# Attention value products of a two-block fp32 kernel: values as weights in split fp32r parts, probabilities moving, outputs with features on partitions

## The reference

```python
h = rmsnorm_2(x, attn_norm_g)
fq, fk, fv, f_logit, sq, sk, sv = split(h @ w_in)     # 8 + 8 heads of width 64
# forgetting attention, causal (s <= t)
p = softmax(q @ k.T / 8 + F[t] - F[s]);  o_fox = p @ v
# stick-breaking attention, strictly causal (s < t)
w = sigmoid(z) * prod_{s<j<t}(1 - sigmoid(z[t,j]));  o_sb = w @ v
o = concat(rmsnorm_2(o_fox, fox_out_g), rmsnorm_2(o_sb, sb_out_g))
x = x + o @ w_out
...
```

## Time and profile before

| | us |
|---|---|
| median of 3 runs | 2620.15 (2619.35 to 2623.75) |
| the profiled execution's own time | 2620.05 |
| span of its profile | 2618.1 |
| busy PE / DVE / ACT / POOL | 2566.8 / 1386.6 / 974.7 / 821.0 |

### The profile page before, as it was taken

How to read it: one execution, slowest core, us unless ns; L and a number is a source line. 1 busy time by engine, 2 the same in 40 slices (tenths; PEclk the granted TensorE clock), 3 DMA queues, 4 the chain that set the end, 5 groups by cost and what they waited for, 6 DMA issues and landing times. The chain is left out here.

```text
span 2618.1 us, 32424 instructions
## 1 busy us (share of the span) xinstructions
PE 2566.8 (98%) x12922; PEld 2135.6 (82%) x12922; DVE 1386.6 (53%) x1285; ACT 974.7 (37%) x1376; POOL 821.0 (31%) x339
## 2 busy tenths in 40 slices
PE   8999999999999999999999999999999999999999
PEld 4888888888788888888888888887888888888887
DVE  5864557656666753544735455465864314431454
ACT  3410044434254420023556556564144213321334
POOL 3565443433344335542111011034422222222230
PEclk9999999999999999999999999999999999999999
DMA  8222221212121153341110111131111111111111
GB/s 328 89 87 71 99 89 57 74 52 65 61 81 61 67 197 123 96 145 65 34 41 33 41 41 34 40 120 58 49 48 48 49 48 48 48 49 64 48 57 65
DMA packets 56552, 194.32 MB, mean 74 GB/s; under 512 B 6857, under 2 KB 10825, under 8 KB 55153
## 3 DMA queue, kind: packets, MB, share of 16 engines
q1 hardware_dynamic: 41312, 141.74, 16.5%
q10 hardware_dynamic: 15120, 50.90, 5.5%
HBM read 158.50 MB, written 29.92 MB: 72 GB/s over the span
## 5 line engine op out<-in xcount | busy, mean ns | idle before, releaser
L238 PE MATMUL G<-H_hi,w_hi 128*128 128x512 f32 x1616 | 502.3, 392 | 1.0 <-ACT silu_zB L724 0.7
L269 POOL TENSOR_TENSOR w_lo<-w_raw,w_hi 128x1024 fp32r<-128x1024 f32 x133 | 348.7, 2622 | 491.1 <-ACT w_hi L263 485.2
L238 PE MATMUL G<-H_lo,w_hi 128*128 128x512 f32 x1616 | 497.7, 389 | 0.0
L238 PE MATMUL G<-H_hi,w_lo 128*128 128x512 f32 x1616 | 497.6, 389 | 0.0
L264 POOL TENSOR_TENSOR w_hi<-w_raw,ones 128x1024 fp32r<-128x1024 f32 x75 | 198.2, 2642 | 593.7 <-PE G L238 472.5
L238 PEld LDWEIGHTS G<-H_lo,w_hi 128*128 128x128 f32 x1616 | 303.3, 188 | 63.4
L238 PEld LDWEIGHTS G<-H_hi,w_lo 128*128 128x128 f32 x1616 | 303.3, 188 | 63.2
L238 PEld LDWEIGHTS G<-H_hi,w_hi 128*128 128x128 f32 x1616 | 300.7, 188 | 64.4 <-issue 4.5
L1845 POOL TENSOR_TENSOR w_lo<-w_raw,w_hi 128x1024 fp32r<-128x1024 f32 x24 | 60.2, 2507 | 479.6 <-ACT w_hi L2059 479.6
L1952 PEld LDWEIGHTS G<-att_v,probsT 128*128 128x128 f32 x1152 | 146.5, 191 | 21.9 <-ACT probsT L2088 13.1
L1900 PE MATMUL G<-A_hi,w_hi 128*128 128x512 f32 x368 | 155.7, 423 | 6.6 <-DVE projected L2238 6.3
(11 more groups left out here) (528 smaller groups left out, 4733.2 us busy)
## 6 DMA issues: line engine op xcount, KB each, us to landing
w_raw<-w_in SPq DMA_DIRECT2D x65, 512.0 KB, 3.6
w_raw<-w_up SPq DMA_DIRECT2D x44, 512.0 KB, 3.6
pre_raw<-w_in SPq DMA_DIRECT2D x30, 512.0 KB, 3.6
wm<-w_mod SPq DMA_DIRECT2D x8, 1024.0 KB, 18.3
w_raw<-w_out SPq DMA_DIRECT2D x16, 512.0 KB, 3.6
w_raw<-w_down SPq DMA_DIRECT2D x16, 512.0 KB, 3.5
xT<-xT SPq DMA_DIRECT2D x8, 512.0 KB, 19.0
b_d<-silu_zB ACTq DMA_DIRECT2D x8, 512.0 KB, 2.6
```

The costliest lines, as they stand in the source:

```text
L238: mm = nc.tensor.matmul(dst[:, n * NB:n * NB + c], w[:, k, :], m[:, k, n * NB:n * NB + c], start=first, stop=last)
L269: nc.gpsimd.tensor_tensor(w_lo[:, slot, 0:kt, :], w_raw[:, slot, 0:kt, :], w_hi[:, slot, 0:kt, :].bitcast(F32), ALU.subtract).then_inc(w_r ...
```

## The change

The value product is turned round. The values of a head are split into a high and a low part of 64 columns each, which together are one 128x128 weight block in fp32r (`VP`); the transposed probabilities are split as well (`pT`, high and low) and move, 256 columns at a time for a pair of query tiles. Rows 0 to 63 of the result are the product with the high values, rows 64 to 127 that with the low values; ACT copies one half and DVE adds the other. The result has features on partitions, so `out_turned` goes. The row sum can no longer be applied to the result, so DVE scales the probabilities of f rounds before they are turned. The squares are made of 64x512 pieces and added up over the rounds; 16 one-column matmuls against ones sum them at the end. `v_turned` moves from the U banks to the score banks, and from step 14 of the round before to step 0 of the round itself. One of the normalisation rows (`R1`) goes to DRAM and comes back at the end to make room.

```diff
@@ pe
-                for c, b0, n in GROUP_AT[g]:
-                    S.wait(pe, "act", "p copied", c)
-                    for b in range(n):
-                        mm = pe.matmul(V[:, at:at + HD], pT[c % 2][:, b, :], v[:, b0 + b, own_rows(hh)], start=b0 + b == 0, stop=b0 + b == tt)
-                    S.mark("pe", "values", mm, c)
+                order = [(b, n) for b in range(tt) for n in range(2)]
+                order = order[:-1] + [(tt, 0), (tt, 1)] + order[-1:]
+                arrived = -1
+                for b, n in order:
+                    if b // 4 > arrived:
+                        arrived = b // 4
+                        S.wait(pe, "dve", "p low", GROUP_AT[g][arrived][0])
+                    c0 = P if b == tt else 0
+                    mm = pe.matmul(V[:, at + c0:at + 2 * P], VP[:, hh, b, :], pT[n][:, b, c0:2 * P], start=(b, n) == (0, 0), stop=(b, n) == order[-1])
+                S.mark("pe", "values", mm, i)
...
-                if s >= 1:
-                    values(s - 1)
-                if n == 0 and 1 <= q <= ROUNDS:
-                    v_turned(q - 1)
-                if s > TILES and s % TILES == 2:
-                    out_turned(s // TILES - 1)
+                if s >= 2 and s % 2 == 0:
+                    values(s // 2 - 1)
+                if 0 <= s < STEPS and s % TILES == 0:
+                    v_turned(s // TILES)
...
             early(0)
-            out_turned(ROUNDS - 1)
+            S.wait(pe, "dve", "squares added", STEPS // 4 - 1)
+            for x in range(2):
+                for t in range(TT):
+                    mm = pe.matmul(S2[:, x * NB + t:x * NB + t + 1], SQ[own_rows(x), t * P:(t + 1) * P], ones[own_rows(x), 0:1], start=True, stop=True)
+            S.mark("pe", "heads summed", mm)
@@ act
+            def out_half(j):
+
+                _, hh, cols = out_at(j)
+                S.wait(act, "pe", "values", 2 * j + 1)
+                if j % 4 == 0 and j:
+                    act.wait_ge(o_stored[out_row(j // 4 - 1)], 16)
+                S.mark("act", "out half", act.activation(OT[own_rows(hh), cols], V[other_rows(hh), :], ACT.Copy), j)
+
+            def square(j):
...
+                S.mark("act", "square", act.activation(dst, OT[own_rows(hh), cols], ACT.Square), j)
@@ dve
+            def made(g):
+                x, _, tt = tile_of(g)
+                w = (tt + 1) * P
+                p, n = pr[g % 2][:, 0:w], g % TILES
+                if x == "f":
+                    S.wait(v, "act", "exp", g)
+                    do("row sum", v.reciprocal(rs[:, n:n + 1], rs[:, n:n + 1]), g)
+                    me("row sum", g)
+                    do("made", v.tensor_scalar(p, p, rs[:, n:n + 1], None, ALU.mult), g)
+                else:
                     S.wait(v, "act", "taken", g)
                     me("first", g)
                     do("made", v.tensor_tensor(p, p, left[:, T - w + 1:T + 1], ALU.mult), g)
 
+            def p_low(g):
+                cols = slice(g % 2 * P, g % 2 * P + P)
+                for c, b0, n in GROUP_AT[g]:
+                    S.wait(v, "act", "p high", c)
+                    do("p low", v.tensor_tensor(pT[1][:, b0:b0 + n, cols], blocks_of(bank_of_u(("p", c)), n), pT[0][:, b0:b0 + n, cols].bitcast(F32), ALU.subtract), c)
+
+            def v_low(r):
...
+            def out_of(j):
...
+                S.wait(v, "act", "out half", j)
+                do("out", v.tensor_tensor(OT[rows, cols], V[rows, :], OT[rows, cols], ALU.add), j)
+
+            def add_squares(j):
...
+                do("squares added", v.tensor_tensor(SQ[rows, cols], SQ[rows, cols], sqt[rows, :], ALU.add), j)
...
+                if 0 <= s + 1 < STEPS:
+                    first(s + 1)
+                if s >= 1:
+                    p_low(s - 1)
+                if s >= 1 and s % TILES == 1:
+                    v_low(s // TILES)
                 if s >= 5 and s % 4 == 1:
-                    out_of((s - 5) // 4)
+                    out_of(s // 4 - 1)
+                if s >= 7 and s % 4 == 3:
+                    add_squares(s // 4 - 1)
                 if 0 <= s + 1 < STEPS:
-                    chain(s + 1)
+                    made(s + 1)
```

214 lines of the change are left out of this document (106 added, 108 removed).

## The result

The changed kernel takes 2665.88 us (median of 4 runs, 2665.14 to 2671.87) against 2620.93 of the kernel before (4 runs, 2619.35 to 2623.75): a ratio of 1.0178, interval 1.0165 to 1.0190, some 45 us more. The forecast was 2644, +24. The direction and the order of the stages came out; the size is nearly twice the one given.

What follows compares the result with a forecast made beforehand. PE was taken to set the pace before, with DVE becoming the bound in s rounds. S rounds +16, f rounds -8, last round +14 and the end +2 gave +24 on 2620.05: 2644 us, range 2614 to 2678.

Steps and rivals of the forecast that it cites:

- S rounds, +4 each: Four s rounds: DVE's work becomes the bound, 76 us against 72.0 each, bounds +1 and +8; +16 in all.
- the clock fall as a rival: Last round: PE works in bursts and drops to 1.2 GHz, +8 on the forecast, 2652 us; chance 0.04.
- F rounds, 69 us each: Three f rounds: a new DVE-ACT chain per tile, 69 against 71.7 us, -2.8 each; -8 in all.
- The last round, +14: Last attention round, without projection pieces: longer chain and scalings held by POOL, +14 us, bounds +5 and +28.
- The chain, +6: Last round: chain through the tiles with squares, splits and final low parts takes about 54 us against 47.8, +6.
- Low parts and outputs lie under the exponential: F rounds: DVE's low parts and outputs run during ACT's exponential, so they add nothing to the 45 us chain.
- The holds, +8: Last round: DVE's scalings wait for POOL's current instruction; eight narrow tiles and three wide, +3 and +5 us.
- The end, +2: After attention: one-column sums +2.7 and slower-clock matmuls +1.6, about half hidden in existing waits; +2, bounds 0 and +4.
- DVE keeps up: All rounds: slack averages out, s rounds 69, f rounds 64.5, last round 50 us; -32, 2588 us; chance 0.14.
- It evens out: All rounds: s rounds +1, f rounds -5, last round +8, within noise; chance 0.05.
- POOL holds more: Last round: each of 14 scalings loses 1.6 us and more; f rounds gain nothing; +46, 2666 us; chance 0.20.
- The matmuls don't get cheaper: Value matmuls: 0.23 us each, PE needs 8 us a round more; about +56, 2676 us; chance 0.05.

Runs made afterwards that it cites:

- x4: Changed kernel without DVE's scaling of the probabilities in f rounds, the reciprocal kept: 2645.41 us, ratio 1.0100.
- y4: Changed kernel with the scaling of the probabilities in f rounds moved from DVE to ACT: 2676.30 us, ratio 1.0214.
- x3: Changed kernel making, from the second round on, only 16 of 128 columns of each low part of the probabilities: 2642.51 us, ratio 1.0083.
- z4: Changed kernel without scaling in f rounds and with POOL splitting only 128 of 1024 columns in the last round: 2643.96 us, ratio 1.0091.
- x2: Changed kernel with POOL splitting only 128 of 1024 columns of the seven early output tiles in the last round: 2657.90 us, ratio 1.0143.
- y2: Changed kernel with POOL's last-round splits cut to 128 of 1024 columns, plus eight spare matmuls before each value product of s rounds and last round: 2657.37 us.
- z1: Changed kernel with four spare matmuls of 256 columns before each value product of the last round only: 2664.33 us, ratio 1.0171.
- z2: Kernel before, with values and transposed probabilities in fp32r, high parts alone, so each value matmul is one pass: 2570.85 us, ratio 0.9818.
- y3: Changed kernel without low parts of the probabilities, 320 value matmuls instead of 640: 2589.68 us, ratio 0.9885.
- x1: Changed kernel with four spare matmuls of 512 columns a step in the last round, before the probabilities are turned: 2670.75 us, ratio 1.0186.
- z3: Changed kernel with DVE's product or scaling of the next tile put before the low parts instead of behind them: 2787.98 us, ratio 1.0640.

## Why the prediction was right in sign and short in size

Two steps failed. The sum has no term for the clock, which the s rounds pay; and in the last round it lets the low parts lie under ACT's exponential, while PE stands there and waits for them. Of the 28 us between the forecast (+24) and the profiled execution (+52), 16 lie in the s rounds, 13 in the last round and 1 in the f rounds; the end has 0, and the earlier start gives 3 back. By the medians the miss is 21.

**PE's side** was right. Value matmuls are 0.12 us apart (1452.16 to 1452.28), 640 of them. PE had to lose its place as the bound, and did: in the s round it is busy 66.7 of 77.2 us by the profile, against 69.1 of 72.0.

**DVE in s rounds**: right. 68.0 us forecast; the durations in the round from 1388.9 add up to 68.4. The profile's 64.5 is less because a record can overlap the next (the scan of 1449.54, above, ends at 1451.30, the low part starts at 1451.21), so busy time is the smaller number. The low parts of 512 columns take 0.68 us, taken as 0.69 from the earlier trace rows.

**S rounds, +4 each**: at full clock the later ones would be 75.5 us, +3.5 on 72.0, by the steps above. Measured were 77.2, 79.9 and 81.6. What failed is that the sum has no term for the clock in s rounds. The forecast had 63 us of work for PE in a round of 76, so 13 us of waits, and had the clock fall as a rival, but for the last round alone and with a chance of 0.04, because "in these rows the clock fell after one-column matmuls only". That sentence was false of the trace: the wait of 2.32 us in the first round, above, was there to be read, and a table by stretch of the kernel before, which I had and did not put among, gives 0.98 for 1255 to 1322. Had I asked what came before each low stretch of the clock, the rival would have become a term; its size was not to be had from one such row. By the estimate of 75.5 the clock costs 1.7 + 4.4 + 6.1 us in the three later s rounds and some 2 in the first: 14 of the 16 us that s rounds have above the +16 forecast.

**F rounds, 69 us each**: 69.2, 69.5 and 69.9. Right, and for the reason given: the chain through the tile sets them (x4 shortens the round by up to 3 us, y4 lengthens it by 4), the low parts lie beside it (x3: nothing). But the scaling and two of the handovers were 11 us of that chain (16 x 0.71), and x4 wins at most 3 without the scaling: that the total came out is in part luck.

**The last round, +14**: measured +27.3. Three parts.
- The chain, +6: with POOL quiet and the clock at 0.97 the round takes 59.6 us, +13. The failed step is "Low parts and outputs lie under the exponential": true of f rounds, where x3 finds nothing, false of the last, where it finds 9.0 us (clock included). With no pieces of the projection between, PE stands at each value product until the low part is there (21.5 us in nine waits), and the low part stands behind the next sum. The scaling's part was counted too high (11 us, z4 against x2: 4.3), so what low parts and waits add is more than the difference of 7. I carried a statement about a covered stage into one without cover.
- The holds, +8: DVE is busy 10.0 us more because of them, so the size of the hold was nearly right, the scalings were held, as said, and low parts escape; the squares, which the forecast did not name, are held too. The profiled rounds differ by 12.6 us, clock included, the medians by 8.0 (x2) and 13.5 (y2).
- The clock: 0.73. z1's round is 4.4 us shorter with half the time at 1.2 GHz, but not by the clock alone; the forecast gave it to a rival, at 8 us.
The three overlap, and their sum can't be split more finely by these runs.

**The end, +2**: 829.3 against 827.5 us. The number is right, one of its two terms is not. The one-column sums and what follows them:

```profile
1846.70 3.31 PE L2030 MATMUL S<-ones,head_squares 64*128 64x1 f32 x32
...
1851.42 0.62 PE L2022 MATMUL G<-A_hi,w_hi 128*128 128x512 f32 x2
1851.89 0.63 PE L2022 MATMUL G<-A_lo,w_hi 128*128 128x512 f32 x2
```

Two matmuls of 512 columns take 0.47 us here (1851.42 to 1851.89), 0.23 us each: the clock is full, and the +1.6 for a clock that falls behind the one-column matmuls did not come. That the attention starts earlier (2.6 us, and 3.3 to 8.1 in the other kernels with the change) was not forecast, and I have no run on it.

**The rivals.** "DVE keeps up" needed s rounds under 70; the later ones are above 77 (its -32 leaves out the +2 of the end). "It evens out" had the last round at +8 and f rounds at -5; neither came. "POOL holds more" gave 2666, the measured number, by luck and another path: it had f rounds gain nothing (they gain 7) and no clock. "The matmuls don't get cheaper" is refuted by 0.12 us. The clock was the one that was needed, in more places than its text named.

## What to carry to other kernels

- When a change takes PE out of the bound, add a term for the clock wherever PE will wait several us for another engine, in every stage; ask what stood before each low stretch that the trace of before already has. Here one such row stood there: a wait of 2.32 us, then 3.4 us at 1.2 GHz.
- What is hidden in one stage has to be asked again for each stage with less beside it: the same low parts, made an eighth as wide, give back 0, 4 and 9 us in three kinds of round (the 9 with a better clock).
- Before work is moved to another engine to make an operation cheap, look for a form that is cheap where it is: the old layout with one-pass operands gave 48 us (z2), the new one with the low parts of the probabilities left out 31 (y3). Both are less exact, and z2 leaves out the low parts of the values too.

## What the runs showed of the hardware that I had not expected

- One and the same wait of 3.28 us goes with 3.4 us at 1.2 GHz in one round and with 6.8 in another, and a wait of 2.3 us with 3.4 us (the kernel before) or none (z2). Rounds with the same work differ by 3 us with it (78.6 at 0.96, 81.6 at 0.92). Executions of one kernel differ by 7 to 9 us (2665.14 to 2671.87; x1 from 2664.08 to 2673.47), and in these two kernels the faster ones have the higher mean clock (0.982 to 0.983 against 0.980; x1 0.988 against 0.985).
- The share of a whole round in which PE is busy does not tell whether the clock falls: z2's last round keeps 1.00 with PE busy 32.6 of 40.4 us, y3's second round has 0.93 at 62.8 of 68.7.
- A scaling on DVE of 128 columns, 0.29 us alone, took 2.05 us beside POOL: what counts is when POOL's instruction ends, not how wide DVE's is. The Trainium skill (GPSIMD Engine Reference, 1. Specifications) has VectorE and GpSimd share their interfaces to SBUF and contend for them when an instruction of DVE has two SBUF inputs or runs in a mode that uses two ports. The squares (two inputs, 2.38 us) and the scalings (2.45) agree, and low parts, which read PSUM and SBUF, stayed at 0.68 in the mean.
- Order on one engine can outweigh work: z3 moves nothing between engines and costs 122 us against the change.
